# Load, first norm, gates and projection of a hybrid encoder step: four stages become one, and the norm's root moves behind the product

## The reference

```
h = x * rsqrt(mean(x*x, axis=-1) + EPS) * norm_g
proj = h @ w_in                       # 1024 -> 4096 (q,k,v) + 2048 (z) + 16 (b) + 16 (a)
qkv, z, b, a = split(proj)
conv = silu(conv over 4 frames of qkv, with 3 rows of history)
q, k = l2norm(q) * DK**-0.5, l2norm(k)
beta = sigmoid(b);  g = -exp(a_log) * softplus(a + dt_bias)
gb = cumsum(g) in chunks of 64 frames
```

## Time and profile before

| | us |
|---|---|
| median of 3 runs | 5150.5 (5149.27 to 5151.6) |
| the profiled execution's own time | 5139.61 |
| span of its trace | 5138.3 |
| PE busy in the span | 4537.8 (88%) |
| DVE, ACT, POOL busy | 1878.8, 1621.6, 976.7 |
| mean granted TensorE clock | 0.92 of full speed |

### The profile page before, as it was taken

How to read it: one execution, slowest core, us unless ns; L and a number is a source line. 1 busy time by engine, 2 the same in 40 slices (tenths; PEclk the granted TensorE clock), 3 DMA queues, 4 the chain that set the end, 5 groups by cost and what they waited for, 6 DMA issues and landing times. The chain is left out here.

```text
span 5138.3 us, 94405 instructions
## 1 busy us (share of the span) xinstructions
PE 4537.8 (88%) x38337; PEld 4273.2 (83%) x38337; DVE 1878.8 (37%) x2917; ACT 1621.6 (32%) x3026; POOL 976.7 (19%) x863
## 2 busy tenths in 40 slices
PE   5899997999887899979859788669999999999994
PEld 4789997888787899979836566669999999999993
DVE  3455404666522100011122322234445454455554
ACT  2573212333322000022200322334344444444442
POOL 0334323444332222313200001310000000000001
PEclk6899998999999899999979656889999999999997
DMA  1222225454242222134120000275556666676675
GB/s 43 63 67 89 93 89 123 99 118 99 59 139 63 75 71 63 59 107 121 56 58 14 1 0 26 75 198 158 158 160 176 173 186 176 171 202 179 177 208 197
DMA packets 975328, 563.49 MB, mean 110 GB/s; under 512 B 139201, under 2 KB 941346, under 8 KB 975090
## 3 DMA queue, kind: packets, MB, share of 16 engines
q1 hardware_dynamic: 909570, 486.33, 34.2%
q10 hardware_dynamic: 55344, 46.60, 3.2%
q0 software_dynamic: 10176, 27.19, 1.9%
HBM read 481.79 MB, written 77.93 MB: 109 GB/s over the span
## 5 line engine op out<-in xcount | busy, mean ns | idle before, releaser
L2220 DVE TENSOR_TENSOR experts_w_lo<-experts_raw,experts_w_hi 128x1024 fp32r<-128x1024 f32 x352 | 415.9, 1222 | 157.5 <-ACT experts_w_hi L2152 157.5
L209 PE MATMUL experts_pa<-experts_hx,experts_w_hi 128*128 128x272 f32 (+5 forms) x1408 | 410.4, 291 | 8.3 <-DVE experts_w_lo L2220 8.3
L209 PE MATMUL experts_pd<-experts_hid,experts_w_hi 128*128 128x272 f32 (+5 forms) x1408 | 411.2, 292 | 0.0
L209 PE MATMUL experts_pb<-experts_hx,experts_w_hi 128*128 128x272 f32 (+5 forms) x1408 | 408.2, 290 | 3.1 <-DVE experts_w_lo L2220 3.1
L210 PE MATMUL experts_pa<-experts_hx,experts_w_hi 128*128 128x272 f32 (+5 forms) x1408 | 408.7, 290 | 0.0
L211 PE MATMUL experts_pa<-experts_hx,experts_w_lo 128*128 128x272 f32 (+5 forms) x1408 | 408.7, 290 | 0.0
L211 PE MATMUL experts_pd<-experts_hid,experts_w_lo 128*128 128x272 f32 (+5 forms) x1408 | 407.9, 290 | 0.0
L210 PE MATMUL experts_pd<-experts_hid,experts_w_hi 128*128 128x272 f32 (+5 forms) x1408 | 407.7, 290 | 0.0
L210 PE MATMUL experts_pb<-experts_hx,experts_w_hi 128*128 128x272 f32 (+5 forms) x1408 | 407.5, 289 | 0.0
L211 PE MATMUL experts_pb<-experts_hx,experts_w_lo 128*128 128x272 f32 (+5 forms) x1408 | 407.5, 289 | 0.0
L209 PE MATMUL proj_pm<-hT,proj_w_hi 128*128 128x384 f32 (+1 forms) x1152 | 386.4, 335 | 14.6 <-POOL proj_w_lo L527 14.6
(11 more groups left out here) (398 smaller groups left out, 11196.2 us busy)
## 6 DMA issues: line engine op xcount, KB each, us to landing
experts_raw<-in_moe_w SPq DMA_DIRECT2D x352, 512.0 KB, 4.7
experts_raw<-in_moe_w SPq DMA_DIRECT2D x128, 704.0 KB, 5.9
projected<-proj_out SPq DMA_DIRECT2D x48, 544.0 KB, 3.7
proj_w<-in_gdn_w_in ACTq DMA_DIRECT2D x48, 512.0 KB, 4.1
ffnup_w<-in_ffn_w SPq DMA_DIRECT2D x44, 512.0 KB, 5.0
ffndown_w<-in_ffn_w SPq DMA_DIRECT2D x32, 704.0 KB, 4.7
mixout_w<-in_gdn_w_out SPq DMA_DIRECT2D x32, 512.0 KB, 4.0
delta_kkq<-projected SPq DMA_DIRECT2D x102, 128.0 KB, 2.9
```

Source lines behind the costliest of these rows:

```text
L209: pe.matmul(out, as_r(w_hi), as_r(x_hi), start=first, stop=False)
L2220: dve.tensor_tensor(as_r(w_lo[:, x, 0:KD, :]), raw[:, x, 0:KD, :], w_hi[:, x, 0:KD, :], ALU.subtract).then_inc(split[x], 1)
```

## The change

The four stages become one, `front_stage`. The host lays the inputs out as the kernel wants them: `xT` by feature, gains, conv weights, history and router turned, each weight tile contiguous per partition.

- The root is not applied ahead of the product. `hT` holds the halves of x * gain alone; the root `xr` is made beside tile 0 from the same slices, and multiplies each tile as it leaves PSUM. Tile 0 starts with the first slice; sums of squares go into the second PSUM tile.
- DVE empties PSUM for q, k, v (`evict`) and z tiles (`z_evict`, into `acc`), multiplying by `xr`. ACT's `empty` goes; z's silu reads `acc`.
- The gate product has weights as the stationary operand: 72 matmuls of 384 or 320 columns into 32 partitions; nine transposes bring it back to frames. The chain is cut into pieces (`gate_turn`) that stand ahead of the last 12 z tiles.
- SP sends `cols` and the decay rows (three DMAs in place of one) behind the last store of the stage.

```
             @block.sync
+                sp.dma_start(m["gains"][:, :], io["gains"]).then_inc(gain_loaded, 16)
+                for k in range(KD):
+                    sp.dma_start(xT[:, k, :], io["xT"][:, k, :]).then_inc(x_loaded[k], 16)
+                    if k == 2:
+                        sp.dma_start(m["const"][:, :], io["consts"]).then_inc(const_loaded, 16)
...
                         store(i, u, silued)
+                sp.wait_ge(cols_set, PRE + 2)
...
+                for r in (R_GC, R_BETA, R_EGC):
+                    sp.dma_start(m["rows_dram"][r], rows[r]).then_inc(gstored, 16)
...
             @block.tensor
+                def x_sums(j):
+                    pe.wait_ge(x_paired, PRE + j + 1)
+                    for b, (s, n) in enumerate(BLK):
+                        last = pe.matmul(pm[:, 1, b, 0:n], cst(C_ONES), xsq[2 * (j % 2)][:, s:s + n], start=(j == 0), stop=(j == KD // 2 - 1))
+                    last.then_inc(x_summed, 1)
...
+                def gate_turn(j):
+                    if j == 0:
+                        pe.wait_ge(ba_split, PRE + 1)
+                        pe.wait_ge(rooted, PRE + 6 * (NQK // 2))
+                        ba_blocks((0, 1))
+                    elif j == 1:
+                        pe.wait_ge(ba_out, PRE + 1)
+                        ba_blocks((2,))
...
-                product(0, 0)
+                pe.wait_ge(w_split[0], PRE + 1)
+                for k in range(KD):
+                    pe.wait_ge(x_split, PRE + k + 1)
+                    last = piece(0, k)
+                    if k == 0:
+                        pe.wait_ge(const_loaded, PRE + 16)
+                    if k % 2 == 0 and k:
+                        x_sums(k // 2 - 1)
+                last.then_inc(done[0], 1)
+                x_sums(KD // 2 - 1)
+                pe.wait_ge(x_logged, PRE + 3)
                 product(0, 1)
...
+                for j in range(TURNS):
+                    gate_turn(j)
+                    product(LOOPED + j // 2, j % 2)
...
             @block.scalar
-                def empty(i, u):
-                    load_next(i, u)
-                    act.wait_ge(done[u], PRE + i + 1)
...
+                def feed(i, u):
+                    act.wait_ge(w_split[u], PRE + i + 1)
+                    load(i + 1, u)
                     round_next(i + 1, u)
...
+                for k in range(KD):
+                    act.wait_ge(x_loaded[k], PRE + 16)
+                    act.activation(as_r(hT[:, 0, k, :]), xT[:, k, :], ACT.Copy, scale=gain(k)).then_inc(x_rounded, 1)
+                    if k == 0:
+                        round_next(0, 0)
+                    if k >= 4:
+                        act.wait_ge(x_summed, PRE + k // 2 - 1)
+                    act.activation(xsq[k % 4], xT[:, k, :], ACT.Square).then_inc(x_squared, 1)
+                round_next(0, 1)
...
             @block.vector
+                def evict(i, u):
+                    dve.wait_ge(done[u], PRE + i + 1)
+                    dve.wait_ge(conved[u], PRE + i)
+                    dve.wait_ge(kept[u], PRE + i)
+                    dve.tensor_tensor(xpad[:, u, HIST:HIST + 768].rearrange("p (b c) -> p b c", b=2), pm[:, u, 0:2, 0:384],
+                                      xr[:, 0:768].rearrange("p (b c) -> p b c", b=2), ALU.mult)
+                    scaled(xpad[:, u, HIST + 768:HIST + PROMPT], pm[:, u, 2, 0:256], 768, 256)
+                    scaled(xpad[:, u, PADW - SAMPLE:PADW], pm[:, u, 2, 256:320], PROMPT, SAMPLE).then_inc(emptied[u], 1)
```

More of the change, by code:

```diff
@@ L218, in split_weights @@
     eng.tensor_tensor(as_r(w_lo), w, w_hi, ALU.subtract).then_inc(split, 1)
[L221 to L280, removed]
@@ L494, in norms, with ba_blocks @@
                         pe.wait_ge(rooted, PRE + 6 * i + 3 * u + max(b - 1, 0))
[L495 to L498 removed]
+                        pe.matmul(pn[:, (3 * u + b) % 2, 0:n], cst(C_ONES), sq[:, u, c:c + n], start=True, stop=True).then_inc(nsummed, 1)
+                def ba_blocks(blocks):
+                    for k in range(KD):
+                        for b in blocks:
+                            c, n = BLK[b]
+                            last = split_product(pe, pn[0:2 * HV, b % 2, 0:n], wba_hi[:, k, :], wba_lo[:, k, :], hT[:, 0, k, c:c + n], hT[:, 1, k, c:c + n], k == 0, k == KD - 1)
+                    last.then_inc(ba_summed, 1)
@@ L601, in _ @@
+                round_next(0, 1)
+                act.wait_ge(eps_set, PRE + 1)
+                act.wait_ge(x_summed, PRE + KD // 2)
+                for b, (s, n) in enumerate(BLK):
+                    act.activation(xr[:, s:s + n], pm[:, 1, b, 0:n], ACT.Ln, bias=m["eps"][:, :], scale=1.0 / D).then_inc(x_logged, 1)
+                act.wait_ge(x_logged, PRE + len(BLK))
+                act.activation(xr[:, :], xr[:, :], ACT.Exp, scale=-0.5).then_inc(x_rooted, 1)
+                feed(0, 0)
                 silu(0, 0)
@@ new lines, in _ @@
+                dve.memset(m["eps"][:, :], EPS).then_inc(eps_set, 1)
+                for k in range(KD):
+                    dve.wait_ge(x_rounded, PRE + k + 1)
+                    dve.scalar_tensor_tensor(out=as_r(hT[:, 1, k, :]), in0=xT[:, k, :], scalar=gain(k), in1=hT[:, 0, k, :],
+                                             op0=ALU.mult, op1=ALU.subtract).then_inc(x_split, 1)
+                    if k % 2:
+                        dve.wait_ge(x_squared, PRE + k + 1)
+                        dve.tensor_tensor(xsq[k % 4 - 1], xsq[k % 4 - 1], xsq[k % 4], ALU.add).then_inc(x_paired, 1)
@@ L675, in _ @@
                     for u in range(2):
+                        evict(i, u)
                         conv(i, u)
+                with dve.Fori(NC // 2, LOOPED) as i:
+                    for u in range(2):
+                        z_evict(i, u)
+                for j in range(TURNS):
+                    gate_turn(j)
+                    z_evict(LOOPED + j // 2, j % 2)
 STEP = ("KS0", "VT", "OT1p", "GT1p", "SC", "VN0", "KT", "S0", "L0", "OUT0", "x1", "SQ0", "d1", "ON0", "x2", "QG", "d2", "OT0", "KS1", "x3", "GT0", "VN1",
```

330 lines of the change are left out of this document (189 added, 141 removed).

## The result

| | before | changed |
|---|---|---|
| median of 4 runs each, us | 5149.89 | 5020.60 (5016.99 to 5027.78) |
| ratio, 95% interval | | 0.9753, [0.9736, 0.977] |
| profiled execution, us | 5139.61 | 5027.78 |
| first instruction of the next stage, us | 791.97 | 679.71 |

A forecast was written before the change was run, and what follows sets the result against it. PE was taken to mostly wait or work badly in stages ahead of the steady projection, and to be the bound from 410 us. 125.6 + 12.1 - 19 - 4.7 = 114.0 less, 5150.5 - 114 = 5036.5 us; range 5020 to 5060.

The forecast's parts named there:

- Term 1, the start: From the kernel's start to PE's first sum behind tile 2: 67.9 us against 193.5, a gain of 125.6.
- The rival that doubled all of tile 0: Tile 0 at 1.2 GHz: its 20.4 us of PE work double, tile 1 starts 20 us later, 5057 us; chance 0.10.
- Term 2, the boundaries: q and k boundaries: evictions leave ACT's list, period falls from 15.41 to 14.6 us, a gain of 12.1 over 15 boundaries.
- The weights are late next: Within q and k: after the evictions leave ACT, the next weights' load ends late, so the period settles at 14.6 us.
- the bound of 20.6: Upper bound of the q and k gain: the wait of 1.37 us gone at 15 boundaries.
- Term 3, v and z: v and z tiles: PE is the bound and gets the same matmuls, so a change of 0.
- Term 4, the gates: Gate work inside z tiles: product 12.0 us, short operations 5, changes of work 2, a loss of 19 (15 to 26).
- Term 5, the end: End of the stage: last z tile through DVE then ACT, SP's DMAs behind its store, a loss of 4.7 (2 to 6).
- The rival with DVE as the bound: Eviction and convolution on DVE overrun q, k and v tiles: 5263 us with e at 10; chance 0.02.
- 32e - 93: Us lost if DVE needs e us more per tile: q and k tiles overrun from e = 2.2, v tiles from 3.6.

The follow-up runs named there:

- control groups: The changed kernel run twice more without an edit, the second time on a third chip: medians 5034.86 and 5028.62 us, next stage at 679.57 and 679.79 us.
- the dummies' experiment: Twelve matmuls of constants added on PE ahead of the first slice, against the changed kernel: next stage at 674.71 us.
- four evictions: DVE writes the first two thirds of each of 32 evictions four times, against the changed kernel: next stage 713.34 us, median 5062.61 us.

## Why the prediction was right

It held, in sign, in mechanism and in nearly every term. Two things were luck. The first median, 5020.60, lies only 0.6 us inside the range, because that group of runs was quick behind the changed part; the control groups (5034.86 and 5028.62) lie well inside. And that the sum is 1.8 us off hides larger errors that cancel: 3.3, 0.9 and 1.1 us too favourable in terms 1, 2 and 5, 3.5 too unfavourable in term 4. By its own steps:

- **Term 1, the start: 125.6 expected, 122.3 measured** (193.50 to 71.19). Two slips of it are found. The first DMA goes out at 3.75, not at 1.75 as taken from the earlier trace rows: the new stage has 63 semaphores to increment instead of 8, and 32 more of them cost 1.24 us there, of which 0.72 is left at the sums behind tile 2. And tile 0's first slices ran at the low clock, which the sum took as 1.00: 1.5 us by the dummies' experiment. The 1.00 near 10 us in the earlier trace rows, weighed there as a reading, is none: that trace's first record of the clock stands at 26.6 us. The rival that doubled all of tile 0 was wrong in length, right in kind; tile 1 begins low again behind the 2.90 us of idle time (0.66 at 42 to 44 us).
- **What the 122 us consist of**, which the prediction left in one piece: hardly the early product (2.7 us at the first sums, 1.6 at the end) and not the weights' layout (0.01 at the sums behind tile 2; its 1.65 us lie in term 2). What is left is that the slices arrive by feature at about 410 GB/s, and the transposes, the norm's own stage and the serial gates no longer stand ahead of tile 0, whose product starts at 16.33 instead of 151.41. This is read from the two traces; no run undoes one of these alone, so how the time divides among them is not shown.
- **Term 2, the boundaries: 12.1 expected, 220.6 - 209.4 = 11.2 measured.** "The weights are late next" was right, and so was the mean period (14.6 expected, 14.70 measured), but not its form: one boundary in two is late, by a table load that stands behind a wait. With the order on ACT turned, the period is 13.78, 1.63 under the old one: the bound of 20.6, counted from the 1.37 of idle time that the earlier trace rows show, should have been 24.5. A wait cost PE 0.26 us more here than the trace shows idle.
- **Term 3, v and z: 0 and 0.** PE is busy 202.90 of 202.90 us.
- **Term 4, the gates: a loss of 19 expected, 159.5 - 144 = 15.5 measured.** The product took its 12; the short operations 3.5 instead of 7. No turn made PE wait, and the chain that is hidden is 12.6 us long when it isn't.
- **Term 5, the end: 4.7 expected, 12.7 - 6.9 = 5.8 measured**: 4.15 us from the last store's issue to that of the last row, and 5.9 from there to the next stage. Sent earlier, they give 4.1 us back.
- Together 122.3 + 11.2 - 15.5 - 5.8 = 112.2, against 114.0.
- **The rival with DVE as the bound** did not come, but its price was wrong: 32e - 93 says that 2.2 us of room lie in a q or k tile, so that 2.97 us more would cost 0.8. They cost 2.1, about 1.2 of it in waits and the rest in the clock that was low along with them; the room is there at one boundary in two only. Busy time is not the measure: silu, square and the next weights' load wait for the convolution, and they end the boundary. For v nothing was lost, as worked out.

## What to carry to other kernels

An engine with idle time in every period can still set the period: ask what is queued, on another engine, behind the thing that it ends. Where an engine's list holds both an operation that others wait for and one with a whole period of room, put the first first; and put loads of the next data where nothing late stands ahead of them. Here the two moves together were worth 13.6 us, more than all that the change itself won at these boundaries. And a wait of PE can cost more than its length: in three places the granted clock was low where PE waited longer (0.96 in the mean with the gates one behind the other, 0.95 with four evictions, 0.88 in tile 1), and PE worked 3.8, 12.7 and 1.7 us longer for the same matmuls.

## What was not expected

- A wait may stand ahead of a table load in one unrolled half of a loop and behind it in the other, by the order in which waits are written; it kept 1.28 us of ACT's work behind the wait in every pair of tiles. How much of this PE sees goes with when the load lands in these runs: idle times of 0.6 us in the run where it took 3.4 us, of 0.8 to 1.2 where it took 3.6 or 3.7.
- The clock column is no witness until the first record of the clock: 5 matmuls in 1.67 us and 12 in 2.00 stand under the same 1.00.
- The time behind the changed part differs by 13 us between executions of the same instructions, the mean granted clock with it; its cause stays open.
